# Fused attention in a streaming encoder step: score blocks ordered by a running budget and by due time, a third buffer of attention weights, and gate operands loaded per output group

## The chip, the core and the metric

The kernel runs on one core of a Trainium2 chip. The metric is the time of one execution on the device in microseconds (us). Three executions of the kernel before took 1441.84, 1443.09 and 1448.96 us; the median is 1443.09 us.

## What is computed

One layer of a hybrid encoder for 2048 prompt frames and 64 new frames of a second stream that has 128 cached frames. All of it is float32. The part that the change touches is forgetting attention, 8 heads of 64 channels (F is a running sum of a learned log forget gate), and the gate behind it:

```python
s = jnp.einsum('bqhd,bkhd->bhqk', qi, k, preferred_element_type=jnp.float32) * sc
s = s + (Fi[:, :, :, None] - Ft[:, :, None, :])
s = jnp.where(kpos[None, :] <= qpos[:, None], s, -jnp.inf)
pr = jax.nn.softmax(s, axis=-1)
return jnp.einsum('bhqk,bkhd->bqhd', pr.astype(v.dtype), v)
...
z = jnp.concatenate([attn * jax.nn.silu(ag), pool * jax.nn.silu(pg)], axis=-1)
return x + gate[:, None, :] * (z @ w_out)
```

## The kernel before

The program has stages, one behind the other: projections (until 679 us of the span), attention (`stage_attend`, until 1225 us) and the output projection (`stage_out`). Precision is kept by splitting operands in a high and a low part (`qa`/`qb`, `ka`/`kb`, `whi`/`wlo`), so most products are two matmuls.

**Steps.** Attention has 32 steps, for each head the four query groups c = 3, 2, 1, 0 of 512 frames (step index 4h + 3 - c). "h5c3" is group 3 of head 5. Queries of group c see keys up to their own frame, so a step has score blocks of 128 queries by up to 512 keys: 16 for c = 3, then 12, 8 and 5 (the fifth is the new stream's). A row of blocks is one tile of 128 queries. The step's second half is a list of units, one for each 128 keys: 16, 12, 8 and 6.

**A score block** (`"score"`): TensorE (PE) makes two matmuls (L1334, L1335), and one for the mask at a row's end (L1337), into one of 3 banks `sps`; VectorE (DVE) copies it to the step's weight buffer and takes the maximum (L1404). At a row's end DVE reduces the maxima (L1409, `"row_max"`), then ScalarE (ACT) takes the exponential of the row in pieces of 1024 (L1378, `"exp"`). When all rows of a step have theirs, DVE inverts the sums (L1430, L1434, `"den"`).

**A unit** (`"turn"`, `"low"`, `"value"`): PE transposes four 128x128 tiles of weights (L1350) into one of 3 banks `tps`, ACT copies them to `whi` (L1384), DVE makes `wlo` (L1414), and three units later PE multiplies both with the values (L1362). At a step's end (`"out"`) ACT and DVE put the result in `att`.

**Order.** `attention_events` writes one list, and every engine works through it in that order. While the units of a step run, the blocks of the next step are put between them: `span = len(st.units) - 3`, so 12 blocks over 13 units under c = 3, 8 over 9, 5 over 5, but 16 over 3 under c = 0. Weights alternate between two buffers, `wx` for odd c and `wy` for even c, so a step's first block waits for the last transpose of two steps ago (the `t_full` wait before L1404).

**SyncE (SP)** issues all transfers of this stage from one queue, in a loop over the steps: `rec_out` stores the inverted sums of the step to HBM (L1271, L1274); for the second head of a pair `gate_in` waits until they have landed and reads them back, broadcast over partitions, in `rb` (L1287); under c = 3 of head h the q and k of head h + 1 are loaded (`load_qk`, L1253, ten transfers), once all blocks of head h - 1, whose buffers they take, are done, and then its values (`load_v`, L1259, L1261); then `gate_out` stores the gated result of the step before (L1294), once GpSimd (POOL) has made it (L1446 to L1455). A wait in this loop holds back everything behind it. PE waits for `qk_in` at the first block of each head.

Of the kernel before, what the change touches and what calls it, by code (L numbers as in the profile page):

```python
# [12 lines left out]
P = 128  # L13
# [1101 lines left out]
def front_share(st, done, want):  # L1115

    ev = []
    for blk in st.blocks[done:want]:
# [6 lines left out]
def exps_of(st, row):  # L1125
    return [("exp", p) for p in st.pieces if p.row == row]


def attention_events():


    ev = []
    late = []
    vals = 0

    def values(upto):
        nonlocal vals
        out = []
        while vals < upto:
            u = UNITS[vals]  # L1140
            out.append(("value", u))
            if u.last:
                out.append(("out", u.out))
            vals += 1
        return out

    def front(st, done, want):
        nonlocal late
        share = front_share(st, done, want)
        ev.extend(late)  # L1150
        late = []
        for kind, blk in share:
            ev.append((kind, blk))
            if kind == "row_max":
                late += exps_of(st, blk.row)

    first = STEPS[0]
    for done in range(len(first.blocks)):
        front(first, done, done + 1)
    ev += late  # L1160
    late = []
    ev.append(("den", first))
    for i, st in enumerate(STEPS):
        nxt = STEPS[i + 1] if i + 1 < len(STEPS) else None
        done, total = 0, len(nxt.blocks) if nxt else 0
        span = max(1, len(st.units) - 3)
        for n, u in enumerate(st.units):
            ev.append(("turn", u))
            want = min(total, -(-total * (n + 1) // span))
            if nxt:  # L1170
                front(nxt, done, want)
            done = want
            if u.i >= 1:
                ev.append(("low", UNITS[u.i - 1]))
            ev += values(u.i - LAG + 1)
            if nxt and n == len(st.units) - 1:
                ev += late
                late = []
                ev.append(("den", nxt))
    ev.append(("low", UNITS[-1]))  # L1180
    return ev + values(len(UNITS))


EVENTS = attention_events()


def stage_attend(nc, io, keep, dram):
# [4 lines left out]
    with Scope(nc, "att") as s:  # L1192
# [6 lines left out]
        wy = s.sb("wy", [P, 4, 1536])  # L1199
        whi = [s.sb(f"whi{n}", [P, 512], F32R) for n in range(W_RING)]  # L1200
# [7 lines left out]
        rb = s.sb("rb", [P, T])  # L1208
        ag = s.sb("ag", [P, T])
# [8 lines left out]
                 "den_sum", "rec_ok", "ag_in", "g_mul", "g_hi", "g_z", "g_lo")  # L1218
        (s_full, s_free, row_ok, exp_ok, t_full, hi_ok, lo_ok, val_ok, low_out, out_ok,
         den_sum, rec_ok, ag_in, g_mul, g_hi, g_z, g_lo) = (s.sem(n) for n in names)  # L1220
# [9 lines left out]
        def weights(st, row):  # L1230

            if row == NQ:
                return wy[0:DEC, 0, 512:512 + DEC + PAST]
            return (wx if st.c % 2 else wy)[:, row % 4, :]

        def rows_done(st):

            return sum(sum(b.last for b in x.blocks) for x in STEPS[:st.index + 1])
# [28 lines left out]
        def rec_out(sp, st):  # L1267

            sp.wait_ge(rec_ok, st.index + 1)
# [6 lines left out]
        def gate_in(sp, st):  # L1276
# [91 lines left out]
        def _(act):  # L1368
            for kind, x in EVENTS:
                st = x.step if kind != "den" else x  # L1370
                e = st.e
                if kind == "exp":
                    act.wait_ge(row_ok, rows_done(st) - sum(b.last for b in st.blocks) + 1
                                + [b.row for b in st.blocks if b.last].index(x.row))
                    if x.i == st.pieces[0].i and st.index >= 8:
                        act.wait_ge(rec_ok, st.index - 8 + 1)
# [18 lines left out]
        def _(dve):  # L1395
            rows = 0
            for kind, x in EVENTS:
                st = x.step if kind != "den" else x
                e = st.e
                if kind == "score":  # L1400
                    dve.wait_ge(s_full, x.i + 1)
                    if x is st.blocks[0] and st.index >= 2:
                        dve.wait_ge(t_full, STEPS[st.index - 2].units[-1].i + 1)
# [20 lines left out]
                elif kind == "den":  # L1424
                    r = slice(4 * x.c, 4 * x.c + 4)
                    dve.wait_ge(exp_ok, x.pieces[-1].i + 1)
# [10 lines left out]
        def _(pool):  # L1437
            for out in OUTS:
# [5 lines left out]
                pool.wait_ge(ag_in, 16 * (pair + 1))  # L1444
                pool.wait_ge(rb_in[n % 2], 32 * (n // 2 + 1))
                pool.tensor_tensor(ag[:, cols], ag[:, cols], rb[:, cols], ALU.mult).then_inc(g_mul, 1)  # L1446
# [4 lines left out]
                pool.tensor_tensor(hi, ag[:, cols], att[:, cols], ALU.mult).then_inc(g_hi, 1)  # L1451
                pool.tensor_tensor(rb[:, cols], ag[:, cols], att[:, cols], ALU.mult).then_inc(g_z, 1)
# [183 lines left out]
```

## Time and profile before

| | us |
|---|---|
| three executions | 1441.84, 1443.09, 1448.96 |
| median | 1443.09 |
| the profiled execution's own time | 1446.99 |
| its span | 1445.2 |
| attention stage, first score matmul to the last gated store issued | 703.1 to 1223.2 |
| PE busy | 1296.9 (90%) |
| DVE busy | 719.2 (50%) |
| ACT busy | 566.9 (39%) |

A busy PE is not a PE at its peak: its records overlap, and a matmul at half clock counts as busy too. So the prediction reads pitches (from the start of one instruction to the start of the next of its kind) and stretches, not busy shares.

### The profile page before, as it was taken

Reading aid. Unit: us, or ns where it says so; the run is one execution under the profiler, and the core shown is the slowest. Engines: PE = TensorE matmul, PEld = TensorE weight load, DVE = VectorE, ACT = ScalarE, POOL = GpSimd, SP = SyncE. Lnnn points to the kernel's source line nnn. Section 1 sums busy time; section 2 is a strip of 40 time slices with the busy share of each in tenths; the row PEclk is TensorE's granted clock in tenths of the full one; section 3 lists DMA queues with packets and bytes.
Section 4 is the critical chain, followed back from the end, with each engine's and each line's share of the span. In section 5 each row is a group of like instructions: output and inputs, shape, how many; then the busy total and the mean of one; then the engine's idle time right before and its main releaser. Section 6 shows DMA issues by size and latency. Waiting matters only on the chain. (4 is left out here: it accounts for less than half of the span.)

```text
span 1445.2 us, 19347 instructions
## 1 busy us (share of the span) xinstructions
PE 1296.9 (90%) x7007; PEld 1047.6 (72%) x7007; DVE 719.2 (50%) x1979; ACT 566.9 (39%) x1152; POOL 179.6 (12%) x196
## 2 busy tenths in 40 slices
PE   3799999999999999998499999999999991599996
PEld 0369988888888888887376776767667671488884
DVE  1436632435463211100388888888887781334434
ACT  2236531222121211111277677767767671211111
POOL 1113310110010101010000230121023024000000
PEclk9899999999999999999599999999999996799998
DMA  9336454122113434312931747719356412855662
GB/s 374 144 110 190 161 162 142 36 76 89 59 46 132 139 124 130 121 59 65 208 57 16 141 66 153 134 46 177 77 106 115 98 30 81 269 163 180 205 197 87
DMA packets 159628, 179.51 MB, mean 124 GB/s; under 512 B 34057, under 2 KB 123517, under 8 KB 154862
## 3 DMA queue, kind: packets, MB, share of 16 engines
q1 hardware_dynamic: 149982, 152.81, 40.6%
q10 hardware_dynamic: 9120, 23.89, 5.0%
q8 instruction: 56, 0.92, 0.3%
q0 software_dynamic: 432, 1.57, 0.3%
q14 instruction: 38, 0.31, 0.1%
HBM read 111.55 MB, written 66.69 MB: 123 GB/s over the span
## 5 line engine op out<-in xcount | busy, mean ns | idle before, releaser
L594 PE MATMUL prj_acc<-prj_hhi,til_whi 128*128 128x512 f32 (+1 forms) x800 | 285.7, 357 | 0.0
L596 PE MATMUL prj_acc<-prj_hlo,til_whi 128*128 128x512 f32 (+1 forms) x800 | 283.7, 355 | 0.0
L595 PE MATMUL prj_acc<-prj_hhi,til_wlo 128*128 128x512 f32 (+1 forms) x800 | 283.5, 354 | 0.0
L1384 ACT ACTIVATE att_whi<-att_tps 128x512 fp32r<-128x512 f32 x336 | 169.3, 516 | 118.1 <-PE att_tps L1350 115.1
L1414 DVE TENSOR_TENSOR att_wlo<-att_tps,att_whi 128x512 fp32r<-128x512 f32 x336 | 190.0, 585 | 32.1 <-ACT att_whi L1384 30.7
L1404 DVE TENSOR_SCALAR_CACHE_REDUCE att_wx<-att_sps 128x512 f32<-128x512 f32 x192 | 113.5, 619 | 130.8 <-PE att_sps L1335 126.5
L1334 PE MATMUL att_sps<-att_ka,att_qa 128*128 128x512 f32 (+4 forms) x328 | 153.5, 468 | 25.5 <-DMA att_kb<-scratch_fkd 23.7
L596 PEld LDWEIGHTS prj_acc<-prj_hlo,til_whi 128*128 128x128 f32 x800 | 150.4, 188 | 21.2
L594 PEld LDWEIGHTS prj_acc<-prj_hhi,til_whi 128*128 128x128 f32 x800 | 150.4, 188 | 20.8
L595 PEld LDWEIGHTS prj_acc<-prj_hhi,til_wlo 128*128 128x128 f32 x800 | 150.5, 188 | 20.7
L1522 PE MATMUL fin_acc<-fin_whi,fin_zh 128*128 128x512 f32 (+1 forms) x272 | 106.8, 392 | 45.2 <-DMA fin_zl<-scratch_z 45.2
L1362 PE MATMUL att_ops<-att_whi,att_vt 128*128 128x512 f32 x336 | 139.9, 417 | 0.0
L1350 PE MATMUL att_tps<-keep_ident,att_wx 128*128 128x128 f32 x672 | 117.6, 296 | 12.3 <-ACT att_wx L1378 7.7
L1335 PE MATMUL att_sps<-att_kb,att_qb 68*128 68x512 f32 (+4 forms) x328 | 126.5, 386 | 0.0
L1362 PE MATMUL att_ops<-att_wlo,att_vt 128*128 128x512 f32 x336 | 124.2, 370 | 0.0
L1350 PEld LDWEIGHTS att_tps<-keep_ident,att_wx 128*128 128x128 f32 x672 | 84.0, 151 | 44.5 <-issue 23.2
L1378 ACT ACTIVATE att_wx<-att_wx,att_nm 128x1024 f32<-128x1024 f32 (+1 forms) x96 | 99.1, 1035 | 29.4 <-DVE att_nm L1409 29.4
L1523 PE MATMUL fin_acc<-fin_wlo,fin_zh 128*128 128x512 f32 (+1 forms) x272 | 106.6, 392 | 0.0
L1524 PE MATMUL fin_acc<-fin_whi,fin_zl 128*128 128x512 f32 (+1 forms) x272 | 106.4, 391 | 0.0
L1334 PEld LDWEIGHTS att_sps<-att_ka,att_qa 128*128 128x128 f32 (+1 forms) x328 | 67.4, 205 | 44.9 <-DMA att_kb<-scratch_fkd 23.9
L957 DVE SCALAR_TENSOR_TENSOR til_olo<-prj_acc,til_ohi 128x512 fp32r<-128x512 f32 (+1 forms) x40 | 23.8, 598 | 152.7 <-ACT til_ohi L778 152.7
L509 POOL TENSOR_TENSOR til_wlo<-til_wraw,til_whi 128x1024 fp32r<-128x1024 f32 x20 | 48.1, 2406 | 406.2 <-ACT til_whi L703 406.2
(181 smaller groups left out, 1916.9 us busy)
## 6 DMA issues: line engine op xcount, KB each, us to landing
til_wraw<-in_w_in SPq DMA_DIRECT2D x20, 512.0 KB, 4.2
att_ka<-scratch_k SPq DMA_DIRECT2D x16, 560.0 KB
scratch_v<-val_vs SPq DMA_DIRECT2D x17, 512.0 KB, 4.4
att_qa<-scratch_q SPq DMA_DIRECT2D x16, 528.0 KB
val_xt<-in_x_prompt ACTq DMA_DIRECT2D x16, 512.0 KB, 4.2
ini_al<-in_w_ada SPq DMA_DIRECT2D x8, 1024.0 KB, 16.0
fin_zh<-scratch_z SPq DMA_DIRECT2D x16, 512.0 KB, 4.2
fin_zl<-scratch_z SPq DMA_DIRECT2D x16, 512.0 KB, 5.6
```

Source lines behind the costliest of these rows:

```text
L594: pe.matmul(out, w[0][:, k, :], hhi[:, k, cs], start=(k == 0), stop=False)
L595: pe.matmul(out, w[1][:, k, :], hhi[:, k, cs], start=False, stop=False)
L596: mm = pe.matmul(out, w[0][:, k, :], hlo[:, k, cs], start=False, stop=(k == KT - 1))
L1334: pe.matmul(bank[0:x.m, 0:x.n], qa[e][:, q], ka[e][:, k], start=True, stop=False)
L1335: mm = pe.matmul(bank[0:x.m, 0:x.n], qb[e][:, q], kb[e][:, k], start=False, stop=not x.last)
L1350: mm = pe.transpose(bank[:, t * P:(t + 1) * P], weights(st, 4 * st.c + t)[:, x.w0:x.w0 + P], keep["ident"][:, :])
L1362: mm = pe.matmul(bank[:, x.skip:x.width], vt[e][0:x.keys, x.tile, :], part[b][0:x.keys, x.skip:x.width], start=(x.first and part is whi), ...
L1384: act.activation(whi[x.i % W_RING][0:x.keys, x.skip:x.width], tps[x.i % T_RING][0:x.keys, x.skip:x.width], ACT.Copy).then_inc(hi_ok, 1)
L1404: dve.tensor_scalar(weights(st, x.row)[0:x.m, x.w0:x.w0 + x.n], sps[x.i % S_RING][0:x.m, 0:x.n], 1.0, None, ALU.mult, ALU.max, accum_out=t ...
L1414: dve.tensor_tensor(wlo[b][0:x.keys, x.skip:x.width], tps[x.i % T_RING][0:x.keys, x.skip:x.width], raw(whi[b][0:x.keys, x.skip:x.width]), ...
L1522: pe.matmul(out, zh[b][:, k, 0:n], whi[:, k, cols], start=(k == 0), stop=False)
L1523: pe.matmul(out, zh[b][:, k, 0:n], wlo[:, k, cols], start=False, stop=False)
```

## The change

1. **Budget and due time.** Rows of blocks ("fronts") stand in one list, sorted by the first unit that needs them. At each unit, blocks are taken from the list while the score columns done so far (`done`) are below 1.12 times the unit columns done so far (`back`), both counted from the first unit. Where the next front in reach has no buffer free yet (`after`), the first that has is taken. Where none has, the unit gets no block. At a step's last unit all blocks that the next step still lacks are put out.
2. **Buffers.** c = 1 gets a buffer of its own, `wz`. So c = 3 and c = 1 wait for the same group of the head before (4 steps ago), c = 2 and c = 0, which share `wy`, for two steps ago (`READY`).
3. **Gate operands.** `ag` and `rb` become two tiles of 512 columns. The load of all of `ag` once per pair goes; `gate_in` loads a piece of `ag` and two of `rb` for each output, and waits for `g_lo` of the output before the last where it waited for `g_mul`.
4. SP's and ACT's counts follow the new order (`DEN_ORDER`, `ROW_ORDER`, `head_blocks`).

```diff
+LEAD = 1.12
+READY = {3: 4, 2: 2, 1: 4, 0: 2}
...
+        self.st, self.row = st, row
+        self.blocks = [b for b in st.blocks if b.row == row]
+        self.pieces = [p for p in st.pieces if p.row == row]
+        self.work = sum(b.n for b in self.blocks)
+        self.after = STEPS[st.index - READY[st.c]].units[-1].i if st.index >= READY[st.c] else -1
+        self.due = st.units[0].i
...
+    waiting = sorted((f for st in STEPS for f in fronts_of(st)), key=lambda f: f.due)
...
+    def exps():
+        nonlocal late
+        for f in late:
+            ev.extend(("exp", p) for p in f.pieces)
+            open_rows[f.st.index] -= 1
+            if open_rows[f.st.index] == 0:
+                ev.append(("den", f.st))
+        late = []
+
...
+    def next_block(turned):
+        nonlocal current
+        if not current:
+            ready = [f for f in waiting if f.after <= turned]
+            if not ready:
+                return None
+            waiting.remove(ready[0])
+            current = [ready[0], list(ready[0].blocks)]
+        return current[1].pop(0)
...
+    done, back = 0, 0
+    for u in UNITS:
+        ev.append(("turn", u))
+        exps()
+        back += u.n * u.keys // P
+        while (waiting or current) and done < LEAD * back:
+            blk = next_block(u.i)
+            if blk is None:
+                break
+            done += blk.n
+            score(blk)
+        nxt = UNITS[u.i + 1] if u.i + 1 < len(UNITS) else None
+        if u.i >= 1:
+            ev.append(("low", UNITS[u.i - 1]))
+        values(u.i - LAG + 1)
+        if nxt and nxt.step is not u.step:
+            while any(f.st is nxt.step for f in waiting) or (current and current[0].st is nxt.step):
+                blk = next_block(u.i)
+                done += blk.n
+                score(blk)
+            exps()
...
-        span = max(1, len(st.units) - 3)
-        for n, u in enumerate(st.units):
-            ev.append(("turn", u))
-            want = min(total, -(-total * (n + 1) // span))
-            if nxt:
-                front(nxt, done, want)
-            done = want
...
+        wz = s.sb("wz", [P, 4, 1024])
...
-        rb = s.sb("rb", [P, T])
-        ag = s.sb("ag", [P, T])
+        rb = [s.sb(f"rb{n}", [P, 512]) for n in range(2)]
+        ag = [s.sb(f"ag{n}", [P, 512]) for n in range(2)]
...
-            return (wx if st.c % 2 else wy)[:, row % 4, :]
+            return {3: wx, 2: wy, 1: wz, 0: wy}[st.c][:, row % 4, :]
...
-            sp.wait_ge(rec_ok, st.index + 1)
+            sp.wait_ge(rec_ok, DEN_ORDER.index(st.index) + 1)
...
-                if st.pair >= 1:
-                    sp.wait_ge(g_lo, n - NS + 1)
                 if n >= 2:
-                    sp.wait_ge(g_mul, n - 1)
+                    sp.wait_ge(g_lo, n - 1)
+                sp.dma_start(ag[n % 2][:, 0:out.width], dram["ag"][st.pair, :, out.cols]).then_inc(rb_in[n % 2], 16)
                 for e in range(2):
-                    sp.dma_start(rb[halves(e)[0], out.cols],
+                    sp.dma_start(rb[n % 2][halves(e)[0], 0:out.width],
...
-            sp.dma_start(ag[:, :], dram["ag"][0]).then_inc(ag_in, 16)
...
-                    sp.wait_ge(s_full, before.blocks[-1].i + 1)
+                    sp.wait_ge(s_full, max(b.i for b in head_blocks(st.head - 1)) + 1)
...
-                    if prev.c == 0:
-                        sp.dma_start(ag[:, :], dram["ag"][prev.pair + 1]).then_inc(ag_in, 16)
...
-                    if x is STEPS[4 * h].blocks[0]:
+                    if x.i == min(b.i for b in head_blocks(h)):
                         pe.wait_ge(qk_in[e], QK * (h // 2 + 1))
...
-                    if x is st.blocks[0] and st.index >= 2:
-                        dve.wait_ge(t_full, STEPS[st.index - 2].units[-1].i + 1)
+                    if x.i == min(b.i for b in st.blocks) and st.index >= READY[st.c]:
+                        dve.wait_ge(t_full, STEPS[st.index - READY[st.c]].units[-1].i + 1)
```

**Where instructions move.** PE at the end of h4c3. Before, in the kernel's own lines: the last transposes of the step (`att_wx`), with value matmuls between, and then the units of h4c2 (`att_wy`), each with blocks of h4c1.

```order
L1362 MATMUL att_ops<-att_whi,att_vt 128x512
L1362 MATMUL att_ops<-att_wlo,att_vt 128x512
L1350 MATMUL att_tps<-keep_ident,att_wx 128x128
L1362 MATMUL att_ops<-att_whi,att_vt 128x512
L1362 MATMUL att_ops<-att_wlo,att_vt 128x512
L1350 MATMUL att_tps<-keep_ident,att_wy 128x128 x4
L1334 MATMUL att_sps<-att_ka,att_qa 128x512
L1335 MATMUL att_sps<-att_kb,att_qb 128x512
```

Now, at the same place: behind the step's last transpose stand 16 blocks, all of h5c3, before the next value matmul; of these the first four and the mask are shown.

```order
L1399 MATMUL att_ops<-att_whi,att_vt 128x512
L1399 MATMUL att_ops<-att_wlo,att_vt 128x512
L1387 MATMUL att_tps<-keep_ident,att_wx 128x128
L1371 MATMUL att_sps<-att_ka,att_qa 128x512
L1372 MATMUL att_sps<-att_kb,att_qb 128x512
L1371 MATMUL att_sps<-att_ka,att_qa 128x512
L1372 MATMUL att_sps<-att_kb,att_qb 128x512
L1371 MATMUL att_sps<-att_ka,att_qa 128x512
L1372 MATMUL att_sps<-att_kb,att_qb 128x512
L1371 MATMUL att_sps<-att_ka,att_qa 128x512
L1372 MATMUL att_sps<-att_kb,att_qb 128x512
L1374 MATMUL att_sps<-keep_mask,keep_identb 128x128
```

The first of these 16 reads q and k of head 5; in the kernel before the first such block stood under h4c0, two steps later. Over the whole list, runs of 5 or more blocks without a transpose between are 6, 5 and 5 under each c = 0 before; now from head 4 on they are 16, 5, 8 and 12 (behind c = 3, 2, 1 and 0), and in these heads nearly all units stand without a block. In heads 0 and 1 most units have one.

SP at the end of an odd head (h1c0 up to the loads for head 3), before:

```order
L1271 DMA scratch_rden<-att_rec 128x4x1 [waits att_rec_ok]
L1274 DMA scratch_rden<-att_rec 64x1
L1287 DMA att_rb<-scratch_rden 64x512 [waits att_g_mul,att_rd_out1,att_rd_out0]
L1287 DMA att_rb<-scratch_rden 64x512
L1287 DMA att_rb<-scratch_rden 64x64 [waits att_g_mul]
L1287 DMA att_rb<-scratch_rden 64x64
L1294 DMA scratch_z<-att_zhi 128x512 [waits att_g_lo]
L1294 DMA scratch_z<-att_zlo 128x512
L1271 DMA scratch_rden<-att_rec 128x4x1 [waits att_rec_ok]
L1253 DMA att_qa<-scratch_q 64x2112 [waits att_s_full]
```

Now, at the same place:

```order
L1312 DMA scratch_rden<-att_rec 128x4x1 [waits att_rec_ok]
L1315 DMA scratch_rden<-att_rec 64x1
L1325 DMA att_ag<-scratch_ag 128x512 [waits att_g_lo,att_rd_out1,att_rd_out0]
L1327 DMA att_rb<-scratch_rden 64x512 x2
L1325 DMA att_ag<-scratch_ag 128x64 [waits att_g_lo]
L1327 DMA att_rb<-scratch_rden 64x64 x2
L1334 DMA scratch_z<-att_zhi 128x512 [waits att_g_lo]
L1334 DMA scratch_z<-att_zlo 128x512
L1312 DMA scratch_rden<-att_rec 128x4x1 [waits att_rec_ok]
L1294 DMA att_qa<-scratch_q 64x2112 [waits att_s_full]
```

Two loads of `ag` are added, and the second output's load waits for `g_lo` of the first's predecessor; the loads of q and k stay behind all of it.

## Rows read from the trace of the kernel before

**Rows 1.** Busy time by stretch: head 1, head 7 (us; engines; clock; DMA share; GB/s).
```profile
780.00:842.00 62.00, 57.70 (x325) 44.06 (x324) 50.70 (x154) 44.94 (x101) 14.21 (x12) 0.94 0.54 104
...
1149.00:1201.00 52.00, 48.24 (x289) 38.16 (x287) 42.17 (x121) 37.23 (x85) 11.23 (x9) 0.96 0.21 37
```
**Rows 2.** The same view, inside head 1: c = 3, 2, 1, 0.
```profile
780.00:802.00 22.00, 21.34 (x120) 17.33 (x119) 18.09 (x51) 16.06 (x38) 1.30 (x1) 0.89 0.51 96
802.00:817.00 15.00, 13.95 (x91) 10.96 (x88) 12.50 (x35) 10.79 (x21) 3.81 (x3) 1.00 1.06 183
817.00:826.00 9.00, 8.43 (x56) 6.39 (x55) 7.68 (x26) 7.12 (x19) 0.00 (x1) 1.00 0.30 65
826.00:842.00 16.00, 13.98 (x66) 9.38 (x65) 12.43 (x45) 10.97 (x23) 9.10 (x8) 0.92 0.24 65
```
**Rows 3.** Timeline of PE in h1c3, a unit with one block.
```profile
791.20 0.60 PE L1350 MATMUL att_tps<-keep_ident,att_wx 128*128 128x128 f32 x4
...
792.59 0.60 PE L1350 MATMUL att_tps<-keep_ident,att_wx 128*128 128x128 f32 x4
```
**Rows 4.** Timeline of PE at the end of h1c2, a unit without a block.
```profile
813.42 0.60 PE L1350 MATMUL att_tps<-keep_ident,att_wy 128*128 128x128 f32 x4
...
814.38 0.52 PE L1350 MATMUL att_tps<-keep_ident,att_wy 128*128 128x128 f32 x3
```
**Rows 5.** Timeline of DVE in h0c0, blocks back to back, with one row's end.
```profile
771.42 0.69 DVE L1404 TENSOR_SCALAR_CACHE_REDUCE att_wx<-att_sps 128x512 f32<-128x512 f32 x1
...
772.04 0.69 DVE L1404 TENSOR_SCALAR_CACHE_REDUCE att_wx<-att_sps 128x512 f32<-128x512 f32 x1
...
773.25 0.42 DVE L1404 TENSOR_SCALAR_CACHE_REDUCE att_wx<-att_sps 128x256 f32<-128x256 f32 x1
...
773.78 0.68 DVE L1404 TENSOR_SCALAR_CACHE_REDUCE att_wx<-att_sps 128x512 f32<-128x512 f32 x1
```
**Rows 6.** Timeline of SP's queue (start, length of the issue), head 1 and into head 2.
```profile
790.20 1.23 SPq L1253 DMA_DIRECT2D att_qa<-scratch_q  x2
...
797.13 15.24 SPq L1261 DMA_DIRECT2D att_vt<-scratch_v  x2
812.42 0.59 SPq L1271 DMA_DIRECT2D scratch_rden<-att_rec  x1
822.04 1.11 SPq L1287 DMA_DIRECT2D att_rb<-scratch_rden  x2
...
835.77 0.49 SPq L1271 DMA_DIRECT2D scratch_rden<-att_rec  x1
...
849.95 2.38 SPq L1287 DMA_DIRECT2D att_rb<-scratch_rden  x4
...
854.82 1.21 SPq L1253 DMA_DIRECT2D att_qa<-scratch_q  x2
...
861.52 21.08 SPq L1261 DMA_DIRECT2D att_vt<-scratch_v  x2
```
**Rows 7.** Waits of SP's queue between 700 and 1230 us (total, times, longest).
```profile
SPq L1285 <- DMA scratch_rden<-att_rec: 132.9, 14, 13.1
```
**Rows 8.** Timeline of PE, the first transpose behind the 16 blocks of h0c3.
```profile
718.84 1.12 PE L1350 MATMUL att_tps<-keep_ident,att_wx 128*128 128x128 f32 x4 [2.02 <-ACT att_wx L1378]
```
**Rows 9.** Timeline of DVE and POOL, an output and its gate (two stretches).
```profile
1197.48 0.69 DVE L1422 TENSOR_TENSOR att_att<-att_ops,att_tmp 64x512 f32<-64x512 f32 x1 [0.39 <-ACT att_tmp L1392]
...
1201.37 1.26 POOL L1451 TENSOR_TENSOR att_zhi<-att_ag,att_att 128x512 fp32r<-128x512 f32 x1
...
1204.00 1.26 POOL L1455 TENSOR_TENSOR att_zlo<-att_rb,att_zhi 128x512 fp32r<-128x512 f32 x1
```
**Rows 10.** Busy time by stretch, around the stage's start.
```profile
679.00:703.00 24.00, 0.47 (x4) 0.24 (x2) 0.00 (x0) 1.70 (x2) 0.00 (x0) 0.57 0.87 170
703.10:718.80 15.70, 13.70 (x36) 10.27 (x36) 10.84 (x36) 8.07 (x15) 0.00 (x0) 0.50 1.09 218
718.80:723.40 4.60, 4.56 (x17) 3.96 (x18) 1.89 (x7) 2.00 (x4) 0.00 (x0) 0.50 1.00 216
```

More of the change, by code:

```diff
@@ L1112, with __init__, fronts_of, attention_events @@
 LAG = 3
-def front_share(st, done, want):
-    ev = []
-    for blk in st.blocks[done:want]:
+LEAD = 1.12
+READY = {3: 4, 2: 2, 1: 4, 0: 2}
+class Front:
+    def __init__(self, st, row):
+        self.st, self.row = st, row
[4 more added lines that the diff above has]
+        self.due = st.units[0].i
+def fronts_of(st):
+    rows = []
+    for b in st.blocks:
+        if b.row not in rows:
+            rows.append(b.row)
+    return [Front(st, row) for row in rows]
+def attention_events():
+    ev, late = [], []
+    vals = 0
+    waiting = sorted((f for st in STEPS for f in fronts_of(st)), key=lambda f: f.due)
+    open_rows = {st.index: len(fronts_of(st)) for st in STEPS}
+    current = []
+    def values(upto):
+        nonlocal vals
+        while vals < upto:
+            u = UNITS[vals]
+            ev.append(("value", u))
+            if u.last:
+                ev.append(("out", u.out))
+            vals += 1
+    def exps():
[6 more added lines that the diff above has]
+        late = []
+    def score(blk):
+        nonlocal current
         ev.append(("score", blk))
@@ L1121, in front_share @@
             ev.append(("row_max", blk))
-    return ev
[L1125 to L1165, printed above, removed]
-        span = max(1, len(st.units) - 3)
-        for n, u in enumerate(st.units):
-            ev.append(("turn", u))
-            want = min(total, -(-total * (n + 1) // span))
-            if nxt:
-                front(nxt, done, want)
-            done = want
[L1173 to L1181, printed above, removed]
@@ L1184 @@
-EVENTS = attention_events()
+            late.append(current[0])
+            current = []
+    def next_block(turned):
+        nonlocal current
+        if not current:
[5 more added lines that the diff above has]
+        return current[1].pop(0)
+    while waiting and waiting[0].st.index == 0:
+        for _ in range(len(waiting[0].blocks)):
+            score(next_block(-1))
+        if len(late) == 2:
+            late, keep_last = late[:1], late[1:]
+            exps()
+            late = keep_last
@@ new lines, in attention_events @@
+    exps()
+    done, back = 0, 0
+    for u in UNITS:
+        ev.append(("turn", u))
+        exps()
+        back += u.n * u.keys // P
[14 more added lines that the diff above has]
+                score(blk)
+            exps()
@@ new lines, in attention_events, with head_blocks @@
+    ev.append(("low", UNITS[-1]))
+    values(len(UNITS))
+    return ev
+EVENTS = attention_events()
+for _n, _b in enumerate([x for kind, x in EVENTS if kind == "score"]):
+    _b.i = _n
+for _n, _p in enumerate([x for kind, x in EVENTS if kind == "exp"]):
+    _p.i = _n
+ROW_ORDER = [(x.step.index, x.row) for kind, x in EVENTS if kind == "row_max"]
+DEN_ORDER = [x.index for kind, x in EVENTS if kind == "den"]
+def head_blocks(h):
+    return [b for st in STEPS[4 * h:4 * h + 4] for b in st.blocks]
@@ L1233, in weights @@
                 return wy[0:DEC, 0, 512:512 + DEC + PAST]
-            return (wx if st.c % 2 else wy)[:, row % 4, :]
-        def rows_done(st):
-            return sum(sum(b.last for b in x.blocks) for x in STEPS[:st.index + 1])
+            return {3: wx, 2: wy, 1: wz, 0: wy}[st.c][:, row % 4, :]
         def gates(out):
@@ L1372, in _ @@
                 if kind == "exp":
[L1373 to L1376, printed above, removed]
+                    act.wait_ge(row_ok, ROW_ORDER.index((st.index, x.row)) + 1)
+                    if x.i == min(p.i for p in st.pieces) and st.index >= 8:
+                        act.wait_ge(rec_ok, DEN_ORDER.index(st.index - 8) + 1)
                     w = weights(st, x.row)[0:x.m, x.w0:x.w0 + x.n]
@@ L1425, in _ @@
                     r = slice(4 * x.c, 4 * x.c + 4)
-                    dve.wait_ge(exp_ok, x.pieces[-1].i + 1)
+                    dve.wait_ge(exp_ok, max(p.i for p in x.pieces) + 1)
                     if x.c == 3 and x.head >= 2:
@@ L1443, in _ @@
                 hi, lo = zhi[n % 2][:, 0:out.width], zlo[n % 2][:, 0:out.width]
-                pool.wait_ge(ag_in, 16 * (pair + 1))
-                pool.wait_ge(rb_in[n % 2], 32 * (n // 2 + 1))
-                pool.tensor_tensor(ag[:, cols], ag[:, cols], rb[:, cols], ALU.mult).then_inc(g_mul, 1)
+                a, r = ag[n % 2][:, 0:out.width], rb[n % 2][:, 0:out.width]
+                pool.wait_ge(rb_in[n % 2], 48 * (n // 2 + 1))
+                pool.tensor_tensor(a, a, r, ALU.mult).then_inc(g_mul, 1)
                 pool.wait_ge(out_ok, out.i + 1)
```

10 lines of the change are left out of this document (5 added, 5 removed).

## Prediction

> **What bounds the kernel now.** Start with the table by stretch. Attention works through its 8 heads evenly: head 1 takes 62 us at a mean clock of 0.94, and the last head 52 us, since it has no blocks of a next head [rows 1]. In a head PE is busy for 57.70 of 62 us, and DVE and ACT for some 50 and 45, so no engine is idle for long. Inside a head the four steps take 22, 15, 9 and 16 us [rows 2]. The last one is the odd one: six units, four of them short, but 16 blocks of the next head under its first three. Next, the timelines give prices. A full unit with a full block takes PE 1.39 us [rows 3], a full unit alone 0.96 [rows 4]. So a block costs PE 0.43 us when it is mixed in. DVE takes a block in 0.62 us when blocks stand back to back, and a row's end adds about 0.19 (0.53 for a 256-column block with its maximum, where 0.34 is its share by size) [rows 5]. Last, SP's queue, which is what a reader skips: it is not busy, but it is a chain. Under the second head of a pair, each step stores its sums, waits until they have landed, and reads them back: 822.04 - 812.42 = 9.6 us for one step, 849.95 - 835.77 = 14.2 for the last one [rows 6]; 132.9 us in 14 such waits [rows 7]. Loads of q and k stand in the same queue.
>
> **What the order becomes.** The first thing to see is in the code. Both counters of the budget run from the stage's start, so "12% ahead" is 12% of everything done so far, not of a step. Unit and block columns of a head are the same number within 1%, so the permitted lead grows by 0.12 head per head, while three buffers hold about one head. From head 4 on the budget never binds, and readiness alone sets the order: the list from the planner shows 16, 5, 8 and 12 blocks at once behind the last transposes of c = 3, 2, 1 and 0, and bare units elsewhere. That is the opposite of even spreading for heads 3 to 6; head 0 and most of 1 are spread as intended.
>
> **Term 1, the order itself.** A head's units alone: 28 full ones at 0.96 = 27; 12 short ones, which I take at 0.5 (half a full one), and two small ones, 7. Together 34 us on PE. Its 45 blocks alone, on DVE: 28 full at 0.62 = 17.4, 12 short ones 4.1, 17 row ends 3.2: 24.9. Each of the four runs leaves an edge: PE then waits for ACT's last exponentials, 2.02 us behind the 16 blocks of h0c3 [rows 8]; I take 4 us for four edges, since behind the short runs three older value products cover it. A bunched head is 34 + 25 + 4 = 63 us against 61.5. Heads 0 and 1, evenly mixed, have PE work of 34 + 45 blocks at 0.43 by size (some 15) = 49 and DVE work of about the same; with the stalls that a mixed stretch shows today (15 us for c = 2, where 12 units and 8 blocks add up to 13.5) I take 58 and 57. The last head has nearly nothing but units: 34 + 4 = 38 where 52 stood. Sum over the stage: 58 + 57 + 62 + 63 + 3 x 63 + 38 = 467 against 482 (718.84, the first transpose, to 1201) [rows 1, 8]: **-15 us**. So if nothing else waited, this would be a small gain; bunching itself is nearly free, because DVE's 0.62 is not far above PE's 0.43.
>
> **Term 2, q and k come too late.** This is the term that decides. Before, the first block of head h + 1 stood under h's c = 0. Now it stands behind h's c = 3, two steps or 24 us earlier. But the load cannot start earlier: it needs head h - 1's blocks done, and it stands in SP's loop behind the waits above. From its first issue to the end of the issues that the full queue holds back it takes 797.13 + 15.24 - 790.20 = 22 us for an even head and 861.52 + 21.08 - 854.82 = 28 for an odd one [rows 6]; I take 22 and 27 until PE can start. Follow a pair in the bunched state, with time zero at the issue for head 5. Landed at 27. Then 16 blocks (12, partly at half clock), the units of h4c2 and 5 blocks (13): 52. Now h4c0's sums exist: store, 14 us, two issues: the load for head 6 leaves at 69 and lands at 91. PE meanwhile does c1 (11), c0 (4), 12 blocks with edge (9) and the units of h5c3 (14), and is there at 90: hardly a wait. Behind the load SP is free at 91, but h5c3's gate comes late, because its last products stand behind the 16 blocks: 101 + 4 for three units, 0.7 each for ACT and DVE and 3.9 for POOL (1201.37 to 1205.26) [rows 9] put it at 110. Then 9.6 and two issues, c2's gate at 123, then 14.2 with six issues: the load for head 7 leaves at about 144 and lands at 171. PE is there at 152: it waits **19 us**. The pair takes 144 instead of 123. The same reckoning from the stage's start, with the steps still mixed, gives waits of about 7 us in head 1 (for head 2), 22 in head 2, 2 in head 3, 18 in head 4, 0 in head 5 and 19 in head 6: **+68 us**. Bounds: had SP's chain its length of today (42.4 us from 812.42 to 854.82) [rows 6] and no gate were late, the three long waits would lose 12 us each, total +32; were the loads also 5 us slower for the added pieces and colder PE stretches, +90.
>
> **Term 3, the clock.** PE's clock is at its lower level (1.2 GHz) for the 15.7 us of the first 16 blocks, which follow 24 us of nearly no matmuls, and for 4.6 us more; it is then at 2.4 GHz, as the first rows of the table by stretch with a clock of 1.00 show [rows 2, 10]. So blocks alone did not bring it back. Behind each of three waits of about 20 us I expect the same: 16 blocks in about 14 us instead of 10, and 2 us on what follows, 6 us each (4 for the 8 blocks in head 2); the short wait in head 1 costs 3. That is 19, and bunches elsewhere may drop it too where today one drop per head is already paid (mean 0.94): I take **+25**, between 5 (only part of it on the chain, since today's drops go) and 50.
>
> **Term 4, gate pieces.** The piece of `ag` adds one issue of about 0.6 us per output, 20 in all, less the 4 whole loads; they lie on SP's chain and are in term 2. At the end, sums of the last step are still stored behind the gate of c = 2, as now (SP chooses no earlier place for it), so the tail stays within **+2 us**. The split tiles and `wz` cost no instruction.
>
> **Sum:** -15 + 68 + 25 + 2 = +80 us. The profiled execution took 1446.99 us, which is 3.9 above the median of the three; the sum goes on the median: 1443 + 80, about **1520 us** (rounded down a little).
>
> **A page against the trace.** The row says 9.6 and 14.2 us from storing sums to reading them [rows 6]. The Trainium skill, page "DMA: Bandwidth & Descriptors", section "Anatomy of one DMA — SWDGE (gpsimd) path", puts the fixed cost of a transfer at some 2 us, mostly for the write's receipt; the stores here leave from SP, another path. By it the chain of one pair would be about 30 us shorter, the load for head 7 would land before PE needs it, and term 2 would nearly vanish, giving rival 1's time. The trace does not agree for this store of single elements, and I go by the rows.
>
> **Rivals.**
> 1. *Loads are in time* (faster). If q and k of head h + 1 landed within 38 us of h4c2's end (c1 11, c0 4, 12 blocks 9, c3 14), term 2 were gone, and with it the long cold stretches: -15 + 0 to 10 = 1428 to 1438, below now. It decides at the first block behind c = 3: the load must leave SP 19 us sooner than I reckon. For it: the sums that SP waits for are ready a step or two earlier than now. Against: the landings that SP waits for are 42 us a pair whatever PE does [rows 6, 7]. Chance 0.08.
> 2. *The wait, but smaller* (SP's chain as today, clock mostly kept): -15 + 32 + 5 + 2 = 1467. Chance 0.2.
> 3. *Half clock for nearly all bunches*: DVE's 0.62 becomes PE's 0.85 per block (15.7 less the edge of 2.0, over 16 blocks) [rows 8, 10], which adds 20 to 25 us and lengthens the chain: 1545. Chance 0.2.
> 4. *The budget works as named* (all heads mixed at about 56 us): some 45 us faster, 1398. The order list excludes it; 0.01.
>
> **How the numbers follow.** The forecast has 0.47, rivals 2 and 3 lie on its side, and 0.04 is for terms 1 to 3 cancelling within 0.5% (7 us, about what a measurement of this kernel can tell from no change). The range from 1463 to 1555 leaves out rival 1, the cancelling case and the tails. Faster 0.09, same 0.04, slower 0.87.
>
> **What would show it.** In the profile after: PE waits for a transfer to `att_kb` in heads 1, 2, 4 and 6, of about 7, 20, 20 and 20 us, each followed by a clock of 0.5; SP's queue issues loads for heads 3, 5 and 7 within 10 us of the start of the head before; units without blocks at 0.96 us; the last head in about 38 us; DVE back to back in the runs. The prediction is wrong if these waits are under 5 us each, or if heads 4 to 6 take less than 65 us on average.

## Result and the profile after

The changed kernel takes 1581.66 us (median of 4 runs, 1575.29 to 1586.04), the kernel before 1442.64 beside it: a ratio of 1.0932, 95% interval 1.0896 to 1.0968, so 139 us slower. Forecast were 1520 us and a range of 1463 to 1555: the direction was right, the size too small, and the time lies above the range. The profiled execution took 1583.11 us (span 1581.4) against 1446.99, which is 136 us to explain. All of it lies in attention: the output stage takes 220 us as before.

The table by stretch of the changed kernel answers [rows 1] (head 1, head 5, and head 7 up to its last transposes) and [rows 2] (head 5 by steps c = 3, 2, 1, 0):
```profile
789.60:869.40 79.80, 62.40 (x333) 47.86 (x334) 53.34 (x165) 46.91 (x101) 14.18 (x12) 0.88 0.45 91
...
1121.50:1199.00 77.50, 65.35 (x323) 49.25 (x322) 52.65 (x153) 46.20 (x98) 15.22 (x12) 0.85 0.46 94
1289.70:1335.00 45.30, 39.20 (x244) 31.86 (x243) 31.27 (x73) 28.83 (x63) 13.79 (x12) 0.95 0.21 47
...
1121.50:1160.30 38.80, 30.72 (x128) 24.16 (x127) 22.66 (x62) 19.12 (x39) 1.27 (x1) 0.70 0.73 145
1160.30:1175.00 14.70, 12.83 (x83) 10.22 (x82) 10.24 (x28) 10.36 (x22) 5.05 (x4) 0.98 0.13 36
1175.00:1186.80 11.80, 10.95 (x63) 7.82 (x62) 9.74 (x30) 8.32 (x20) 5.09 (x4) 1.00 0.41 91
1186.80:1199.00 12.20, 10.85 (x54) 7.04 (x53) 10.01 (x36) 8.40 (x20) 3.80 (x3) 1.00 0.02 1
```
Heads 1 to 6 now take 78 to 91 us each instead of 62, from first transpose to first transpose, and half of head 5 is its c = 3: 38.8 us where 22 stood, at a clock of 0.70 (the share of full speed that TensorE was granted). The changed kernel's waits, by engine (total, times, longest):
```profile
PE att_sps L1371 <- DMA att_kb<-scratch_fkd: 87.4, 7, 23.4
PE att_tps L1387 <- DVE att_wlo L1450: 50.7, 63, 2.2
DVE att_den L1466 <- ACT att_wx L1414: 14.9, 8, 2.4
DVE att_den L1466 <- ACT att_wy L1414: 13.7, 8, 2.8
DVE att_wy L1440 <- remote: 7.4, 2, 5.8
DVE att_rec L1470 <- ACT att_wz L1414: 5.7, 8, 1.3
DVE att_rec L1469 <- ACT att_wy L1414: 4.7, 8, 1.4
```
The first row is q and k: 23.4 us of it is the stage's start, as before; the other six, one in each of heads 1 to 6, are 9.6, 14.6, 7.3, 14.0, 4.2 and 14.2, together 64 us. The next ones are new: DVE waits 39 us in 32 groups for ACT's last exponentials (2.1 us before) ahead of the sums and their inverses, and PE 51 us for the low half of the weights (15.6 before). "remote" is idle time for which the trace names no engine; below it is called a stop. What is not in the waits is the clock: PE's busy time is 1330.1 us for the same 7007 matmuls that took 1296.9, +33.

SP's queue around the load for head 6 (it answers [rows 6]), and SP's waits (it answers [rows 7]):
```profile
1042.66 1.54 SPq L1294 DMA_DIRECT2D att_qa<-scratch_q  x2
...
1071.93 27.62 SPq L1312 DMA_DIRECT2D scratch_rden<-att_rec  x3
1099.59 0.52 SPq L1315 DMA_DIRECT2D scratch_rden<-att_rec  x1
1100.15 0.59 SPq L1312 DMA_DIRECT2D scratch_rden<-att_rec  x1
1123.07 0.33 SPq L1325 DMA_DIRECT2D att_ag<-scratch_ag  x1
...
1124.58 1.24 SPq L1294 DMA_DIRECT2D att_qa<-scratch_q  x2
...
1145.57 0.59 SPq L1312 DMA_DIRECT2D scratch_rden<-att_rec  x1
1154.10 0.35 SPq L1325 DMA_DIRECT2D att_ag<-scratch_ag  x1
...
1205.31 1.16 SPq L1294 DMA_DIRECT2D att_qa<-scratch_q  x2
```
```profile
SPq L1324 <- DMA scratch_rden<-att_rec: 167.6, 14, 22.6
SPq L1312 <- DVE att_rec L1470: 133.2, 8, 28.1
SPq L1334 <- POOL att_zlo L1491: 66.0, 10, 12.8
```
One store of sums by itself still takes 8.5 us (1145.57 to 1154.10). But now three leave within a microsecond: the 512 sums of the even head's c = 0 at 1099.19 (the last of the x3 in the row that starts at 1071.93), its 64 sums of the new stream (L1315), and the 512 of the odd head's c = 3. The last of them is issued at 1100.15 and has landed 23 us later, at 1123.07, and the load for head 6 stands right behind that. From one odd head's load to the next it is 1205.31 - 1042.66 = 163 us.

### The profile page after: what moved, and what is told of

It reads as the page before. It is cut to its first block and busy times, and to the rows that moved or that the text cites. A ratio compares the mean times of both kernels' runs of the same rounds, so it can differ in the third digit from the quotient of the medians.

```text
span 1581.4 us, 19327 instructions
## 1 busy us (share of the span) xinstructions
PE 1330.1 (84%) x7007; PEld 1068.7 (68%) x7007; DVE 728.1 (46%) x1979; ACT 575.2 (36%) x1152; POOL 179.3 (11%) x196
## 5 line engine op out<-in xcount | busy, mean ns | idle before, releaser
L1371 PE MATMUL att_sps<-att_ka,att_qa 128*128 128x512 f32 (+4 forms) x328 | 158.1, 482 | 96.0 <-DMA att_kb<-scratch_fkd 87.4
L1440 DVE TENSOR_SCALAR_CACHE_REDUCE att_wx<-att_sps 128x512 f32<-128x512 f32 (+3 forms) x128 | 79.7, 638 | 198.7 <-PE att_sps L1372 195.3
L1371 PEld LDWEIGHTS att_sps<-att_ka,att_qa 128*128 128x128 f32 (+1 forms) x328 | 73.5, 224 | 125.3 <-DMA att_kb<-scratch_fkd 89.7
L1399 PE MATMUL att_ops<-att_whi,att_vt 128*128 128x512 f32 x336 | 149.5, 445 | 0.0
L1372 PE MATMUL att_sps<-att_kb,att_qb 68*128 68x512 f32 (+4 forms) x328 | 135.2, 415 | 0.0
L1414 ACT ACTIVATE att_wx<-att_wx,att_nm 128x1024 f32<-128x1024 f32 x64 | 67.8, 1061 | 125.3 <-DVE att_nm L1445 124.9
L1387 PE MATMUL att_tps<-keep_ident,att_wx 128*128 128x128 f32 x464 | 80.8, 298 | 26.2 <-DVE att_wlo L1450 23.1
L1387 PEld LDWEIGHTS att_tps<-keep_ident,att_wx 128*128 128x128 f32 x464 | 61.4, 153 | 46.0 <-issue 28.7
```

The costliest lines, as they stand in the source:

```text
L1371: pe.matmul(bank[0:x.m, 0:x.n], qa[e][:, q], ka[e][:, k], start=True, stop=False)
L1372: mm = pe.matmul(bank[0:x.m, 0:x.n], qb[e][:, q], kb[e][:, k], start=False, stop=not x.last)
L1387: mm = pe.transpose(bank[:, t * P:(t + 1) * P], weights(st, 4 * st.c + t)[:, x.w0:x.w0 + P], keep["ident"][:, :])
L1399: mm = pe.matmul(bank[:, x.skip:x.width], vt[e][0:x.keys, x.tile, :], part[b][0:x.keys, x.skip:x.width], start=(x.first and part is whi), ...
```

## Experiments

Each run is told by its ratio to the kernel before as measured beside it, since the kernel before itself moved from one set of measurements to the next (medians 1446, 1450, 1453, 1464, 1468). The theories A, B and C are those of the expectation that stands above each result.

**1. Three parts taken apart.**
```diff
# gates_only: before.py, gate tiles and loads in pieces as in the change, order untouched
# even (after.py)
-        while (waiting or current) and done < LEAD * back:
+        while (waiting or current) and done < min(LEAD * back, back + 512):
# qk_early (after.py): q and k of head h + 2 under c = 1 of head h, ahead of the gates
+                if st.c == 1 and st.head < HEADS - 2:
+                    sp.wait_ge(s_full, max(b.i for b in head_blocks(st.head)) + 1)
+                    load_qk(sp, st.head + 2)
                 if st.e == 1:
                     gate_in(sp, st)
...
-                    sp.wait_ge(s_full, max(b.i for b in head_blocks(st.head - 1)) + 1)
-                    load_qk(sp, st.head + 1)
```


> The kernel before with part 3 of the change alone (ag and rb in pieces of 512 columns, loaded per output; order and buffers as before). Theory A (order and late q/k loads made the change slow): within 0.3% of the kernel before, 1443 +- 4 us, since SP's loads for heads 3, 5 and 7 leave some 3 us later and had about 5 us to spare. Rival (the pieces lengthen SP's chain until PE waits for q and k): 1455 us or more, with PE waiting for att_kb at the c = 0 steps.

> The changed kernel with one edit: q and k of head h+2 are issued under c = 1 of head h, ahead of the wait for the stored sums, once head h's blocks are done. Theory A: the waits for att_kb behind c = 3 (64 us in the six heads) go, and a part of the half-clock time with them (some 15 us); 1500 us +- 10. Rival B (the order itself is what costs, the waits only fill time that DVE's or SP's chain would take anyway): no less than 1550 us, with the idle time moved to other waits.

> The changed kernel with one edit: the budget is also capped at 512 columns ahead, so every head is mixed as head 0 is. The loads stay where they are. Theory A: the bunches go (and with them 40 us of edges and half clock), but q and k of the next head are needed under c = 2, as early as before the edit, so PE still waits 60 to 90 us for them: 1530 to 1560 us. Rival B (bunching is the whole cost): 1450 us or less.

> Both edits. Theory A: no wait for att_kb over 1 us behind the first, no bunches: a head takes some 57 to 60 us, attention 470 to 490 us, total 1425 to 1450 us. Rival B: what is left is DVE's in-order wait for the last exponentials of a step, and the total stays over 1470 us.

Measured: gates_only 1449.68 us, ratio 1.0012 (0.9992 to 1.0032): the pieces cost nothing that can be told from zero. qk_early 1494.80, 1.0318 (1.0271 to 1.0365), by A: the late loads cost 87 us of the 139. That is the 64 us of waits and the 26 us by which PE's busy time falls (1330.1 to 1304.1 us, for the same matmuls), nearly all of what the clock had cost. even 1537.18, 1.0610 (1.0572 to 1.0648), by A. even_qk_early 1477.60, 1.0203 (1.0156 to 1.0250): no wait for q and k is left behind the stage's first, and the lead is capped, and yet it is 2% slower than before. Theory A fell here; its rival B, over 1470 us with DVE's wait for the last exponentials left, came. The waits point at the place:
```profile
DVE att_den L1467 <- ACT att_wy L1415: 14.6, 8, 2.4
DVE att_den L1467 <- ACT att_wx L1415: 13.6, 8, 2.1
```

**2. The place of the inversion.** The timeline of DVE in the changed kernel at the end of h4c0, and then that of PE (start, length, and in brackets the idle time before and its releaser):
```profile
1123.04 0.69 DVE L1440 TENSOR_SCALAR_CACHE_REDUCE att_wy<-att_sps 128x512 f32<-128x512 f32 x1 [1.61 <-remote]
...
1124.06 0.21 DVE L1450 TENSOR_TENSOR att_wlo<-att_tps,att_whi 128x64 fp32r<-128x64 f32 x1
1125.83 0.17 DVE L1466 TENSOR_TENSOR att_den<-att_den 128x4 f32<-128x4 f32 x1 [1.56 <-ACT att_wy L1414]
1126.03 0.18 DVE L1470 RECIPROCAL att_rec<-att_den 128x4 f32<-128x4 f32 x1
1126.13 0.18 DVE L1450 TENSOR_TENSOR att_wlo<-att_tps,att_whi 64x64 fp32r<-64x64 f32 x1
```
```profile
1124.42 0.63 PE L1387 MATMUL att_tps<-keep_ident,att_wx 128*128 128x128 f32 x4 [2.19 <-DVE att_wlo L1450]
1126.46 0.95 PE L1387 MATMUL att_tps<-keep_ident,att_wx 128*128 128x128 f32 x4 [1.27 <-DVE att_wlo L1450]
```
The inversion itself is short (0.17 and 0.18 us), but DVE takes its work in order and stands for it until ACT is done; the `wlo` at 1126.13 stands behind it, and PE's transposes at 1126.46 behind that `wlo` (1.27 us). PE's wait just before, 2.19 us, is not the inversion's: it ends with the `wlo` at 1124.06, which stood behind DVE's stop of 1.61 us. The kernel before had the inversion two to three units later. The edit in `attention_events` (of the kernel before in den_now, of the changed one in the others):
```diff
# den_now (before.py): in front(), right behind the last exponentials
         ev.extend(late)
+        if late and done == len(st.blocks):
+            ev.append(("den", st))
...
-                ev += late
+                if late:
+                    ev += late
+                    ev.append(("den", nxt))
                 late = []
-                ev.append(("den", nxt))
# den_late, qk_den, even_qk_den (after.py); even_qk_den3 with 3
-                ev.append(("den", f.st))
+                dens.append([2, f.st])
...
+        for d in dens:
+            d[0] -= 1
+        while dens and dens[0][0] < 0:
+            ev.append(("den", dens.pop(0)[1]))
```


> The kernel before, with nothing changed but the place of the inversion: right behind the group's last exponentials, as the change has it, where it stood two to three units later. A: waits of VectorE for ScalarE of over 30 us appear and the kernel is 15 to 35 us slower, 1460 to 1480. B: the waits appear, but hidden: 1443 to 1451.

> The changed kernel, but a group's row sums are inverted two units later in the order of the events than its last exponentials (in the changed kernel right behind them). Theory A (VectorE takes its work in order, so the inversion waits there for ScalarE's last exponentials, 39 us in 32 groups in the changed kernel against 2 us before, and the low half of the next weights stands behind it): those waits go; TensorE gets back some 20 to 40 us of them, 1545 to 1565 us. Theory B (the waits lie beside ScalarE's own queue, whose copies stand behind the same exponentials, so TensorE waits as long anyway): 1575 to 1590.

> The changed kernel with both the early loads of q and k and the inversion two units later. A: 1494.8 less 20 to 40, 1455 to 1475. B: 1488 or more. If the two parts add up, its distance to the early loads alone is that of the late inversion alone to the changed kernel.

> Evened order, early loads of q and k, inversion two units later. A: the 32 us left between this order and the kernel before (1477.6 against 1445) are these waits, 35 to 39 us of them here: 1440 to 1455. B: 1470 or more, and the 32 us are the even order's own (shorter steps for groups 1 and 0, where a unit is bound by ScalarE and VectorE).

Measured: den_now 1492.31 us, 1.0307 (1.0264 to 1.0350). One event of each step moved in the order of the kernel before costs 42 us, more than theory A's upper end of 35. Its waits:
```profile
DVE att_den L1433 <- ACT att_wx L1381: 23.2, 8, 3.1
DVE att_den L1433 <- ACT att_wy L1381: 15.8, 8, 2.1
...
PE att_tps L1353 <- DVE att_wlo L1417: 40.0, 50, 2.1
PE att_tps L1350 <- DVE att_wlo L1417: 32.7, 15, 4.2
```
even_qk_den 1434.78, 0.9888 (0.9850 to 0.9926): 3% under even_qk_early, 1.1% faster than the kernel before, and below A's 1440 to 1455. In bunched order it is worth half: qk_den 1475.68, 1.0159 (1.0120 to 1.0198). On the changed kernel alone it is worth nothing: den_late 1589.44, 1.0965 (1.0928 to 1.1001), where A said 1545 to 1565. The time is B's (1575 to 1590), its reason is not seen: DVE no longer waits for ACT there, but the stops grew from 9 us to some 35 (counted once where DVE and ACT stop together), PE's waits for q and k from 87 to 96, and the biggest stop ends with a landing, as the timelines of DVE and then of SP's queue show:
```profile
1277.43 0.08 DVE L1448 DVE_READ_ACCUMULATOR att_wy<-att_sps 128x1 f32 x1
1288.53 0.69 DVE L1448 TENSOR_SCALAR_CACHE_REDUCE att_wy<-att_sps 128x512 f32<-128x512 f32 x1 [11.01 <-remote]
```
```profile
1263.01 0.59 SPq L1320 DMA_DIRECT2D scratch_rden<-att_rec  x1
1288.28 0.33 SPq L1333 DMA_DIRECT2D att_ag<-scratch_ag  x1
```
Three stores issued together are under way from 1262 to 1288, and DVE starts again when they have landed. That the stops took back what the inversion gave is read from these sums; no run here takes them apart in this order.

**3. The stores of the sums.**
```diff
# rows16 (after.py), even_qk_den_rows16
             sp.dma_start(dram["rden"][h, 512 * c:512 * c + 512]
-                         .rearrange("(t p) -> p t", p=P),
+                         .rearrange("(p t) -> p t", t=4),
# even1024_qk_den: even_qk_den with back + 1024
```


> The changed kernel, with the inverse sums of a group written as 128 rows of four numbers, in the order in which they lie in the buffer, where it writes 512 single numbers (so the gates read them in another order: that part of the output is not the reference's). Theory A (the stores of sums are slow because of their single numbers, 8 to 9 us each and 23 us for three, and SP waits 168 us for them, so that the next heads' q and k leave late): three stores land within 8 us, SP's waits for them fall below 80 us, TensorE's waits for q and k from 64 us in six heads to under 35, and the stops of VectorE and ScalarE that the trace puts to no engine (8.6 us) are gone: 1530 to 1560 us. Theory B (q and k leave late because they stand behind the odd head's gates, whose last step comes late in any case): the stores are as short, but the waits for q and k stay above 50 us, 1570 to 1585. Theory C (a store takes its 8 us whatever its rows): nothing moves.

> The same shorter rows on the fastest order so far (evened, early loads, late inversion). There no group waits for q and k after the first, so by A only the stops of 12.5 us go with the stores: 1422 to 1430. If the stops have nothing to do with the stores: 1432 to 1438.

> The evened order with early loads, and the inversion three units late instead of two. If two units are enough to cover ScalarE's last exponentials (no such wait is left in the trace of the run with two), nothing is gained: 1431 to 1441. If the row sums now come too late for the stores and gates, the gate loads and with them the next heads' q and k slip: 1440 to 1450.

> The same as the fastest order, but the score work may run 1024 columns ahead of the turned ones instead of 512 (the changed kernel's 12% lets it run ahead without end, about two steps by head 3). Theory A (running ahead costs by itself, since the blocks then bunch where a group's buffer comes free; 41 us lie between the order with 12% and the evened one): a part of it comes back, 1440 to 1455. Theory B (only a lead of thousands of columns bunches): 1431 to 1439.

Both runs with rows16 in their name leave out the matching order on the reading side, so the gates get the sums in another order and that output is not the reference's; the instructions are the same. Measured: rows16 1500.26 us, 1.0324 (1.0283 to 1.0365). Nothing of the order was touched, and 6% is gone, as much as with the early loads and more than A said (1530 to 1560). These are largely the same microseconds as those of the early loads: with the loads early and the inversion late, short rows take only 16 us off the bunched order (qk_den 1475.68, bunch_all_rows 1459.35, below). SP's waits for landings halve:
```profile
SPq L1334 <- POOL att_zlo L1491: 116.4, 10, 20.0
SPq L1324 <- DMA scratch_rden<-att_rec: 81.8, 14, 9.2
```
Three stores together land in 9.2 us or less (1054.61 to 1064.42 in its timeline, with the issue; the 64 in the middle are still single numbers) instead of 23, PE's waits for q and k in heads 1 to 6 fall from 64 to 11 us, and there is no stop, here and in the six other runs with short rows. Three kernels with single numbers (before, gates_only, even_qk_early) have none either. even_qk_den_rows16: 1425.60, 0.9808 (0.9770 to 0.9846), by A. even_qk_den3: 1437.24, 0.9899 (0.9862 to 0.9936): two units are enough. even1024_qk_den: 1456.04, 1.0019 (0.9989 to 1.0050): 512 columns more lead take back all of the gain, a little more than A said, so it is the running ahead that costs.

**4. What is left of bunching, and the best version.** Here GpSimd's first gate product reads the sums back in their order, which the two runs above leave out:
```diff
+                if out.width == 512:
+                    a3, r3 = a.rearrange("c (t p) -> c t p", t=4), r.rearrange("c (p t) -> c t p", t=4)
+                    pool.tensor_tensor(a3, a3, r3, ALU.mult).then_inc(g_mul, 1)
# bunch_all_rows = qk_den, even_all_rows = even_qk_den, before_rows = before.py, each with short rows
```


> The changed kernel's order (12% ahead of everything done, so bunched from head 3 on), with early loads of q and k, the inversion two units later, and the sums stored in rows of four numbers, which GpSimd reads back in their right order (so the output is the reference's). Theory A (bunching costs by itself: bare units at 0.96 us and runs of blocks at VectorE's pace, with edges): 35 us or more above even_all_rows, 1455 to 1470 us. Theory B (the prediction's: bunches are nearly free, the 41 us seen were the slow stores that collide with them): less than 15 us above it, 1430 to 1442.

> All three corrections (evened order with early loads, inversion two units later, short rows with GpSimd reading them in order). GpSimd's first product of a gate reads a strided operand, which lies beside other work: 1420 to 1430 as with the unordered rows, if the stride costs it nothing on the path; 1430 to 1438 if it does.

> The kernel before with the short rows alone. Theory A (before, no group waits for q and k and no engine stops behind a store, so short stores move only SP's waits): 1440 to 1450, no change. Theory B (the slow stores cost the kernel before too, through the tail of the last step or the clock): 1425 to 1438, and then the fastest version owes its gain to the stores, not to the order.

> The kernel before with short rows, once more. Theory A (nothing gained, the last ratio of 0.987 came from high runs of the kernel before): ratio 0.995 to 1.003. Theory B (a real gain): 0.982 to 0.992.

> All three corrections, once more. By theory A: 0.980 to 0.988 of the kernel before (1427 against 1443 to 1453), and as far under before_rows_again. By theory B the two stand within 0.5% of each other.

Measured: even_all_rows 1426.84 us, 0.9743 (0.9700 to 0.9787), as even_qk_den_rows16 (1425.60), so the strided operand costs nothing that shows; bunch_all_rows 1459.35, 0.9963 (0.9937 to 0.9988); before_rows 1446.21, 0.9873 (0.9821 to 0.9925). So bunches cost 32.5 us with late loads, inversion and stores out of the way, a little under A's 35 and far over B's 15. Once more: even_all_rows_again 1428.94, 0.9737 (0.9716 to 0.9758), before_rows_again 1443.91, 0.9835 (0.9807 to 0.9862). Against before_rows the ratio is B's, and against the kernel before even_all_rows_again lies under A's 0.980 to 0.988. What holds within one set is that the best version is 15 to 19 us (1.0 to 1.3%) under the kernel before with the same short rows; that fits even_qk_den, which is 1.1% under the kernel before without them. What the short rows give the kernel before on their own is less sure. In the profile of before_rows the heads take 61.5 us as before; only the last step with its hand-over is 5 us shorter, and the stage started 4 us later, so the spans are the same (1445.6 and 1445.2). Why the kernel before lies at 1464 and 1468 us in just these two sets, while before_rows does not rise, stays open, and with it how much of the 1.3 and 1.7% is the rows'.

Where the evened order gains is seen in two rows, from 700 to 1200 us of the kernel before and then of even_qk_den: with the waits for q and k and for the inversion out of the way, PE is busy for 438.7 us at a clock of 0.96, where the kernel before needs 461.5 at 0.93 for the same 2568 matmuls.
```profile
700.00:1200.00 500.00, 461.52 (x2568) 351.65 (x2568) 405.69 (x1222) 356.72 (x775) 75.03 (x69) 0.93 0.53 99
700.00:1200.00 500.00, 438.73 (x2568) 340.74 (x2568) 408.63 (x1224) 354.09 (x776) 80.04 (x72) 0.96 0.56 99
```

## Why the prediction was right in kind and wrong in size

**What the order becomes: right.** The counters let the lead grow until readiness decides, and heads 3 to 6 are bunched behind last transposes. even and even1024_qk_den show that this is what costs, not spreading.

**Term 2 (+68): right in sum, in part by luck.** 64 us in six heads, but as 10, 15, 7, 14, 4 and 14 where 7, 22, 2, 18, 0 and 19 were forecast, and with a pair period of 163 instead of 144. Two errors stood against each other: the heads were slower than reckoned, which hides a part of the wait, and SP's chain was longer, which makes it. "Store, 14 us" for the head's last sums was 23, because the odd head's first sums are issued right behind them and SP waits for all three. rows16 confirms that these stores carry the term: with them short, 53 of the 64 us are gone. The fixed cost of 2 us that the Trainium skill gives for transfers issued from GpSimd (page "DMA: Bandwidth & Descriptors", section "Anatomy of one DMA — SWDGE (gpsimd) path") is not what these stores from SP take: 8.5 us for one of single numbers, and 9 for three with rows of four.

**Term 3 (+25): right.** PE's busy time rose by 33 us, and 26 of them went with the waits in qk_early. Behind even the short wait of 4.2 us, in which PE did nothing, all 16 blocks ran at the lower level (timeline of PE, then the table by stretch: clock 1.00 ahead of the wait, 0.50 behind it):
```profile
1141.32 0.27 PE L1387 MATMUL att_tps<-keep_ident,att_wx 128*128 128x128 f32 x1
1145.82 0.79 PE L1371 MATMUL att_sps<-att_ka,att_qa 128*128 128x512 f32 x1 [4.23 <-DMA att_kb<-scratch_fkd]
```
```profile
1135.00:1141.60 6.60, 6.59 (x42) 5.21 (x41) 5.16 (x8) 4.47 (x8) 0.00 (x0) 1.00 1.01 212
1145.80:1159.30 13.50, 13.48 (x37) 10.23 (x37) 9.96 (x32) 6.79 (x12) 0.00 (x0) 0.50 0.44 78
```

**Term 4 (+2): right.** gates_only, 1.0012.

**Term 1 (-15): wrong, and with it the forecast.** Of the 136 us, 64 are term 2, 33 at most the clock, 5 a later start of the stage (708.06 against 703.1 for its first block; between runs of one order it moves as much). That leaves 34 or more where -15 stood: some 50 us. qk_early says the same from the other side: with the late loads gone it is still 49 us above the kernel before. Two things are in it, and besides them 9 us of stops, which I did not foresee at all; the parts are not additive to the microsecond.
- *"Den" moved, and I gave it no price.* The diff puts the inversion right behind the last exponentials. I counted what each engine does, not what stands in line behind an instruction that waits. In the same place it costs the kernel before 42 us (den_now). In the changed kernel head 0 alone loses 5.5 us by it (65.9 us; 60.4 in den_late), and with the loads early, where it shows, the whole kernel 19 (qk_early 1494.80, qk_den 1475.68).
- *"I take 4 us for four edges", "58 and 57" for mixed heads and 38 for the last one were too low.* With loads, inversion and stores mended (bunch_all_rows) heads 0 and 1 take 61 and 62 us, heads 3 to 6 66 on average instead of 63, and the last one takes 45 us in the changed kernel (1289.7 to 1335). The mended version is 13 us slower than before_rows instead of 15 faster: 28 us of the miss. "Bunching itself is nearly free" is the sentence that fell: it costs 32.5 us against the evened order.

**Rivals.** None came. Rival 1 (loads in time) is refuted by the six waits, rival 2 (shorter waits) by their 64 us. Rival 3 (1545, half clock for nearly all bunches) came nearest: PE's busy time rose by 33 us where it needed some 50. The outcome lies beyond all of them because these three contain term 1. Rival 4, the budget as named, was priced at 1398; mended on all three counts it gives 1427.

## What to carry to other kernels

An event that moves in a list takes its wait with it: for every moved instruction ask what stands behind it on its in-order engine, however short it is itself, and keep what closes a group a unit or two behind the work it closes. Cap a running lead by an amount, not by a share of all that was done. Where a queue waits for landings, price what happens when several of them are issued at once, and look at the rows they write before moving anything else.

## What the runs showed of the hardware

- A store of 128 x 4 sums as single numbers takes 8.5 us to land. Together with the 64 sums of the new stream it is 14.2 [rows 6], and with another 512 right behind them 23. With the 512 in rows of four numbers all three take 9 us or less, and one alone 5.9 (rows16, 1086.39 to 1092.25).
- In nine of the twelve kernels with single-number stores DVE or ACT stops for 1 to 11 us with no engine to blame (some 35 us in den_late), mostly until such stores land: DVE at 1123.04 and SP at 1123.07 in the changed kernel. In the seven runs with short rows there is no stop, and none in the kernel before, gates_only and even_qk_early. The cause was not tested; one candidate is the engines' own instruction transfers, for which the profile's page lists DMA queues.
- GpSimd's product of 512 columns with the strided operand takes 1.56 us on average; products of that width without the stride took 1.28.
